# Linear attention: the output is centred through V instead of behind the scan, and the gate's 160 rows are split 80 + 80

## The reference, cut to what matters

```python
def rwkv7_time_mix(h, ...):
    ...
    g = jax.nn.sigmoid(xg @ g1) @ g2          # g1: 1024 x 160, g2: 160 x 1024
    ...                                       # layer 3 alone: v = v + (v_first - v) * sigmoid(v0 + (xv @ v1) @ v2), v1: 1024 x 32
    def step(state, inp):
        r_t, w_t, k_t, v_t, kk_t, a_t = inp
        sa = jnp.einsum('bhvk,bhk->bhv', state, kk_t)
        state = (state * w_t[:, :, None, :]
                 - sa[..., None] * (kk_t * a_t)[:, :, None, :]
                 + v_t[..., None] * k_t[:, :, None, :])
        return state, jnp.einsum('bhvk,bhk->bhv', state, r_t)
    _, y = lax.scan(step, s0, ...)
    mu = jnp.mean(y, axis=-1, keepdims=True)                  # over the 64 values of a head
    var = jnp.mean(jnp.square(y - mu), axis=-1, keepdims=True)
    y = ((y - mu) * lax.rsqrt(var + RW_GN_EPS)).reshape(B, S, D) * ln_w + ln_b
    y = y + (jnp.sum(rh * kh * r_k, axis=-1, keepdims=True) * vh).reshape(B, S, D)
    return (y * g).astype(h.dtype) @ w_out, v_layer
```

## Time and profile before

| | us |
|---|---|
| median of 3 runs | 3857.55 |
| lowest and highest | 3850.71 and 3878.20 |
| the profiled execution's own time | 3843.13 |
| its span, first to last instruction | 3841.3 |

### The profile page before, as it was taken

One profiled execution on the slowest core, in us unless ns is written; L12 is line 12 of the kernel. 1 busy time (PEld: TensorE's weight loads), 2 busy tenths in 40 slices (PEclk: granted clock), 3 DMA queues, 4 the chain that ended last, 5 costly groups with the idle time before them and its releaser, 6 DMA issues.

```text
span 3841.3 us, 90367 instructions
## 1 busy us (share of the span) xinstructions
PE 3685.4 (96%) x34565; PEld 3501.6 (91%) x34565; DVE 1609.5 (42%) x3511; ACT 1892.2 (49%) x2782; POOL 2634.8 (69%) x1186
## 2 busy tenths in 40 slices
PE   8988998999899898899999999999999999999998
PEld 7668997998699766799999999999999999999998
DVE  6643315315642664333221564753223222276442
ACT  5325447544454442545555555455555555545643
POOL 5006873885288400488888878778888988886886
PEclk9999999999999998999999999999999999999999
DMA  6564652664366355466666646557666666664664
GB/s 189 198 215 144 184 171 81 185 192 120 88 186 192 110 177 198 146 203 185 193 192 193 187 143 193 147 146 204 192 193 180 200 186 199 189 183 131 185 184 139
DMA packets 1162942, 664.78 MB, mean 173 GB/s; under 512 B 30157, under 2 KB 1122201, under 8 KB 1162551
## 3 DMA queue, kind: packets, MB, share of 16 engines
q1 hardware_dynamic: 1162679, 661.06, 58.3%
HBM read 659.92 MB, written 1.05 MB: 172 GB/s over the span
## 4 chain that ended last, share of the span: by engine, by line
PE 57%; issue 26%; POOL 12%; DVE 3%; ACT 1%; DMA 0%; POOLq 0%; DVEq 0%; SPq 0%; ACTq 0%
PE bank L866 55%; POOL wlo L626 12%; PE bank L845 1%; DVE bank L3155 1%; PE bank L1067 0%; ACT whi L636 0%; DMA raw<-in_w_in 0%; POOLq L625 0%; PE bank L966 0%; DVE front L2080 0%; POOLq L101 0%; DVE front L2078 0%; PE bank L2796 0%; DVE gains L2669 0%; DVE AB L3169 0%
## 5 line engine op out<-in xcount | busy, mean ns | idle before, releaser
L626 POOL TENSOR_TENSOR wlo<-raw,whi 128x1024 fp32r<-128x1024 f32 (+3 forms) x1182 | 2634.6, 2245 | 1182.6 <-ACT whi L636 1177.1
L636 ACT ACTIVATE whi<-raw 128x1024 fp32r<-128x1024 f32 (+3 forms) x1182 | 1170.7, 995 | 1068.8 <-PE bank L866 904.0
L866 PE MATMUL bank<-AH,whi 128*128 128x256 f32 (+1 forms) x5712 | 1595.9, 279 | 23.5 <-DVE AL L776 9.6
L866 PE MATMUL bank<-AL,whi 128*128 128x256 f32 x5712 | 1588.7, 278 | 0.0
L866 PE MATMUL bank<-AH,wlo 128*128 128x256 f32 (+1 forms) x5712 | 1587.9, 278 | 0.0
L866 PEld LDWEIGHTS bank<-AH,whi 128*128 128x128 f32 x5712 | 1078.5, 189 | 32.5 <-issue 18.9
L866 PEld LDWEIGHTS bank<-AH,wlo 128*128 128x128 f32 x5712 | 1079.5, 189 | 0.0
L866 PEld LDWEIGHTS bank<-AL,whi 128*128 128x128 f32 x5712 | 1077.4, 189 | 0.6
L866 PE MATMUL bank<-HH,whi 128*128 128x256 f32 x1936 | 538.9, 278 | 0.0
L866 PE MATMUL bank<-HH,wlo 128*128 128x256 f32 x1936 | 536.8, 277 | 0.0
L866 PE MATMUL bank<-HL,whi 128*128 128x256 f32 x1936 | 536.8, 277 | 0.0
(11 more groups left out here) (478 smaller groups left out, 4756.5 us busy)
## 6 DMA issues: line engine op xcount, KB each, us to landing
raw<-in_ffn_w SPq DMA_DIRECT2D x420, 512.0 KB, 4.0
raw<-in_w_in SPq DMA_DIRECT2D x182, 512.0 KB, 3.9
raw<-in_ffn_w_gu SPq DMA_DIRECT2D x176, 512.0 KB, 3.8
ada_raw<-in_w_ada SPq DMA_DIRECT2D x96, 512.0 KB, 6.2
raw<-in_ffn_w_down SPq DMA_DIRECT2D x64, 512.0 KB, 3.6
raw<-in_rw_w_rkv SPq DMA_DIRECT2D x48, 512.0 KB, 3.6
raw<-in_w_ada SPq DMA_DIRECT2D x48, 512.0 KB, 6.1
raw<-in_ffn_w SPq DMA_DIRECT2D x56, 384.0 KB, 3.5
```

The lines of the kernel that those rows point to most:

```text
L626: pool.tensor_tensor(wlo[slot][:, 0:n], raw[slot][:, 0:n], whi[slot][:, 0:n], ALU.subtract).then_inc(lo_ready, 1)
L636: act.activation(whi[slot][:, 0:n], raw[slot][:, 0:n], ACT.Copy).then_inc(hi_ready, 1)
L866: mm = pe.matmul(ps[:, 0:o.shape[2]], w, o[:, k0 + c, :], start=tile not in started and c == n == 0, stop=last_panel and c == nk - 1 and n ...
```

## The change

1. V is turned against `CENTRE` in place of the identity, so the scan's outputs come out centred. `CENTRE` is made by DVE just ahead of the scan, and PE waits for it (`centre_made`) ahead of the first chunk. The matmuls of line 1737 and the semaphores `centred` and `centred_taken` go.
2. ACT squares each half of a chunk's output straight from its bank, to `y_squares` (W[5] in layer 0, VF in layer 3): 8 Squares of 128x256 in a layer in place of 4 of 128x512. In chunks 0 to 2 the Square follows the copy, and it is now the Square that raises `y_taken`. In the last chunk it precedes the copy.
3. The sums over heads read these squares, to banks 6, 7, 5 and 4. ACT's order behind the scan becomes: round 0, Ln probe, round 1, Ln x4, Exp x4, round 2, high parts x4, round 3.
4. DVE multiplies `RW_Y`, from SBUF, by the gate, with no wait between the four, and puts this to W[1].
5. The 160 gate rows are split 80 + 80 in all of DMA, both products and the sigmoid. v2's 32 rows move to partitions 96 to 127 beside the first 80.

```diff
-        CENTRED, SPREAD = bank[0:4], bank[4:8]
+        SPREAD = (bank[6], bank[7], bank[5], bank[4])
+        def y_squares(layer):
+            return W[5] if layer == 0 else VF
...
-            sp.dma_start(lg2[:, :], a["rw_g2"][j][0:P, :]).then_inc(lora_landed, 16)
-            sp.dma_start(lgv2[0:32, :], a["rw_g2"][j][P:L_G, :]).then_inc(lora_landed, 16)
+            sp.dma_start(lg2[0:L_G // 2, :], a["rw_g2"][j][0:L_G // 2, :]).then_inc(lora_landed, 16)
+            sp.dma_start(lgv2[0:L_G // 2, :], a["rw_g2"][j][L_G // 2:L_G, :]).then_inc(lora_landed, 16)
...
-            base = {"w": 0, "a": 64, "v": 32, "g": 0}[name]
-            m = min(n, P)
+            base = {"w": 0, "a": 64, "v": 96, "g": 0}[name]
+            m = n if n <= P else n // 2
...
-                    pe.matmul(o, lg2[:, cols], lora_g[:, :], start=True, stop=False)
-                    mm = pe.matmul(o, lgv2[0:32, cols], lora_gv[0:32, :], start=False, stop=True)
+                    half = slice(0, L_G // 2)
+                    pe.matmul(o, lg2[half, cols], lora_g[half, :], start=True, stop=False)
+                    mm = pe.matmul(o, lgv2[half, cols], lora_gv[half, :], start=False, stop=True)
...
-                    act.activation(v3(RW_Y)[...], OUT_BANKS[k][:, h]..., ACT.Copy).then_inc(y_taken if ch < NCH - 1 else head_in, 1)
+                    if ch == NCH - 1:
+                        act.activation(square, o, ACT.Square).then_inc(centre_squares, 1)
+                        act.activation(y, o, ACT.Copy).then_inc(head_in, 1)
+                    else:
+                        act.activation(y, o, ACT.Copy)
+                        act.activation(square, o, ACT.Square).then_inc(y_taken, 1)
...
             act_round(act, out_panels, 0)
             act.activation(log_probe[:, :], eps[:, 2:3], ACT.Ln)
-            squared_pair(0)
-            squared_pair(1)
             act_round(act, out_panels, 1)
-            squared_pair(2)
-            squared_pair(3)
-            act_round(act, out_panels, 2)
             for p in range(4):
                 ... Ln of SPREAD[p]
             for p in range(4):
                 ... Exp of SPREAD[p]
+            act_round(act, out_panels, 2)
...
             pe.wait_ge(scan_in, after(pe, scan_in))
+            pe.wait_ge(centre_made, after(pe, centre_made))
...
-                    turn = crossed(bank[1], of(V), eye, c)
+                    turn = crossed(bank[1], of(V), centred, c)
...
-            pe.wait_ge(centre_made, after(pe, centre_made))
             for p in range(4):
                 if p % 2 == 0:
-                    pe.wait_ge(head_in, after(pe, head_in))
+                    pe.wait_ge(centre_squares, after(pe, centre_squares))
+                if p == 2:
+                    pe.wait_ge(head_in, after(pe, head_in, 2))
                 for c in range(2):
-                    mm = pe.matmul(CENTRED[p][...], CENTRE[:, :], RW_Y[:, cs], start=True, stop=True)
-                mm.then_inc(centred, 1)
-            ... (the sums over heads, from RW_B)
+                    mm = pe.matmul(SPREAD[p][...], const("headones"), y_squares(layer)[:, cs], start=True, stop=True)
                 mm.then_inc(spread_ready, 1)
-            pe.wait_ge(centred_taken, after(pe, centred_taken, 4))
...
-            yc = RW_P
+            yc = W[1]
             for p in range(4):
-                dve.wait_ge(centre_squares, after(dve, centre_squares))
-                dve.tensor_tensor(yc[:, pairs[p]], CENTRED[p][:, :], RW_G[:, pairs[p]], ALU.mult).then_inc(centred_taken, 1)
+                op = dve.tensor_tensor(yc[:, pairs[p]], RW_Y[:, pairs[p]], RW_G[:, pairs[p]], ALU.mult)
```

More of the change, by code:

```diff
@@ L1231, in pe_lora_in @@
                 for c in range(C):
-                    mm = pe.matmul(bank[5][0:n - P, 0:S], w3[:, c, P:n], x[:, c * S:(c + 1) * S],
+                    mm = pe.matmul(bank[5][0:n - m, 0:S], w3[:, c, m:n], x[:, c * S:(c + 1) * S],
                                    start=c == 0, stop=c == C - 1)
@@ L1270, in act_lora_mid @@
             elif name == "v":
-                op = act.activation(lora_gv[32:64, :], bank[4][32:64, 0:S], ACT.Copy)
+                op = act.activation(lora_gv[96:P, :], bank[4][96:P, 0:S], ACT.Copy)
             else:
-                act.activation(lora_g[:, :], bank[4][:, 0:S], ACT.Sigmoid)
-                op = act.activation(lora_gv[0:32, :], bank[5][0:32, 0:S], ACT.Sigmoid)
+                half = slice(0, L_G // 2)
+                act.activation(lora_g[half, :], bank[4][half, 0:S], ACT.Sigmoid)
+                op = act.activation(lora_gv[half, :], bank[5][half, 0:S], ACT.Sigmoid)
             op.then_inc(lora_act, 1)
@@ L1471, in act_rwkv @@
             pairs = [slice(2 * p * S, 2 * (p + 1) * S) for p in range(4)]
-            def squared_pair(p):
-                act.wait_ge(centred, after(act, centred))
-                act.activation(RW_B[:, pairs[p]], CENTRED[p][:, :], ACT.Square).then_inc(centre_squares, 1)
             for slot in range(RING):
@@ L1601, in eye, with centred @@
                     return const("ident")[r, r]
+                def centred(c, r):
+                    return CENTRE[r, r]
                 def keys(c, r):
@@ L1730, in pe_rwkv @@
             pe_scan(pe, layer)
-            pe.wait_ge(centre_made, after(pe, centre_made))
             for p in range(4):
                 if p % 2 == 0:
-                    pe.wait_ge(head_in, after(pe, head_in))
+                    pe.wait_ge(centre_squares, after(pe, centre_squares))
+                if p == 2:
+                    pe.wait_ge(head_in, after(pe, head_in, 2))
                 for c in range(2):
                     cs = slice((2 * p + c) * S, (2 * p + c + 1) * S)
-                    mm = pe.matmul(CENTRED[p][:, c * S:(c + 1) * S], CENTRE[:, :], RW_Y[:, cs], start=True, stop=True)
-                mm.then_inc(centred, 1)
-            for p in range(4):
-                pe.wait_ge(centre_squares, after(pe, centre_squares))
-                for c in range(2):
-                    cs = slice((2 * p + c) * S, (2 * p + c + 1) * S)
-                    mm = pe.matmul(SPREAD[p][:, c * S:(c + 1) * S], const("headones"), RW_B[:, cs], start=True, stop=True)
+                    mm = pe.matmul(SPREAD[p][:, c * S:(c + 1) * S], const("headones"), y_squares(layer)[:, cs], start=True, stop=True)
                 mm.then_inc(spread_ready, 1)
-            pe.wait_ge(centred_taken, after(pe, centred_taken, 4))
             pe_first_tiles(pe, f"rw{layer}.out", FIRST_TILES)
@@ L1921, in dve_rwkv @@
             dve.wait_ge(scan_in, after(dve, scan_in))
+            dve.scalar_tensor_tensor(CENTRE[:, :], const("headones"), -1.0 / DH, const("ident"),
+                                     ALU.mult, ALU.add).then_inc(centre_made, 1)
             dve_scan(dve, layer)
-            yc = RW_P
+            yc = W[1]
             pairs = [slice(2 * p * S, 2 * (p + 1) * S) for p in range(4)]
```

18 lines of the change are left out of this document (7 added, 11 removed).

## The result

| | kernel before | changed kernel |
|---|---|---|
| median of 8 runs each, same chip, us | 3854.72 | 3830.21 |
| lowest and highest, us | 3837.20 and 3878.20 | 3820.42 and 3845.64 |
| the profiled execution's own time, and its span | 3843.13, 3841.3 | 3825.00, 3823.2 |
| mean granted clock of PE | 0.982 | 0.984 |

What follows compares the result with a forecast made beforehand. The prediction took PE to bound the kernel, with 57% of the span on its matmuls. Gate and tail, 2 x (2.75 + 1.4) = 8.3 us, off the median of 3857.55 gave 3849 us, range 3833 to 3866.

Steps and rivals of the forecast that it cites:

- An edit's own place: The gate's expansion, forecast to save 2.75 us a layer, and the tail behind the scan, 1.4 us a layer.
- a place that had been put at zero: The gate's input product: its change of columns from 128 + 32 to 80 + 80 was forecast to gain zero.
- The whole kernel's time: All of the kernel: 8.3 us less than a median of 3857.55, so 3849 us; chance of this forecast 0.55.

## What to carry to other kernels

An edit's own place could be forecast to 0.2 us a layer from the trace: count what is released by what, and move each end. What was missed was a place that had been put at zero, so follow a group to the second instruction behind it, and not only to its own last one. The whole kernel's time couldn't be forecast to better than some 10 us here, since the time at half clock (120 to 140 us in all) differed by 16 us between the two kernels; when a gain of a few tenths of a per cent doesn't match its place, compare the mean granted clock over all runs before looking for a hidden cause, and put the changed kernel itself into every set. And two operands of 80 rows, alternating, took 0.863 us a tile here, where 128 + 32 and 96 + 64 took 1.254.

## What was not expected of the hardware

- Matmuls of 80 rows follow each other every 0.216 us, as those of 128 rows do. Between two shapes of rows 0.20 us are lost each time (128 and 32, 96 and 64), and between two shapes of columns some 0.17 (128 and 32, 96 and 64, against 80 and 80).
- Four products on DVE with two SBUF operands took 6.80 us beside POOL's subtractions and 2.50 without them; POOL's two panels took 5.19 and 4.80. All of DVE's loss falls on the two products that start while POOL is at a panel.
- The same program had medians of 3842.61 to 3860.39 us on five chips, each at another time.
- Matmuls that nobody needs, put into 3.6 us of PE's idle time in each tail, left the first tile's start where it was, 12.94 us behind the placement; the time was 3.1 us longer, with a standard error of 3.1.
